# Token halves of an FFN by tile parity, two products of the second weight tile moved into the entry, and a packed halo for the pooling band

## The reference

```python
for i in range(2):
    hn = rms_norm(h, mix_pre_g[i])
    m = multiscale_pool(hn, pool_w, pool_scale) if i == 0 else attention(hn @ w_q, k, v, sinks) @ w_o
    h = h + rms_norm(m, mix_post_g[i])
    f = swiglu(rms_norm(h, ffn_pre_g[i]), w_gate, w_up, w_down)
    h = h + rms_norm(f, ffn_post_g[i])
    h = h + (p[i] @ w_ple_proj[i]) * sigmoid(rms_norm(h, ple_norm_g[i]) @ w_ple_gate[i])
    if i == 0: k, v = shared K (with rotary) and V from rms_norm(h, kv_norm_g)
```

## Time and profile before

| | us |
|---|---|
| median of 3 runs | 1965.93 (1965.68 to 1967.02) |
| the profiled execution | 1965.92 |
| its span | 1964.1 |
| PE busy in the span | 1917.4 |
| mean granted clock | 0.998 of 2.4 GHz |

### The profile page before, as it was taken

One profiled execution on the slowest core, in us unless ns is written; L12 is line 12 of the kernel. 1 busy time (PEld: TensorE's weight loads), 2 busy tenths in 40 slices (PEclk: granted clock), 3 DMA queues, 4 the chain that ended last, 5 costly groups with the idle time before them and its releaser, 6 DMA issues.

```text
span 1964.1 us, 28703 instructions
## 1 busy us (share of the span) xinstructions
PE 1917.4 (98%) x9198; PEld 1573.6 (80%) x9198; DVE 1402.6 (71%) x2382; ACT 905.4 (46%) x1734; POOL 457.5 (23%) x448
## 2 busy tenths in 40 slices
PE   7899999999999999999999999999999999999998
PEld 7778888888888878888866787788888888888787
DVE  5987777777777786565389658777777777777863
ACT  6744444444444453341178545444444444444531
POOL 2312222222222221010046211212122221222310
PEclk9999999999999999999999999999999999999999
DMA  5333332233333350254200213233333223335201
GB/s 201 108 97 104 91 91 87 76 102 91 107 91 91 92 200 22 78 219 172 86 12 2 66 42 123 71 107 92 98 94 91 86 75 106 91 106 176 99 30 67
DMA packets 222055, 188.50 MB, mean 96 GB/s; under 512 B 12192, under 2 KB 199968, under 8 KB 221984
## 3 DMA queue, kind: packets, MB, share of 16 engines
q1 hardware_dynamic: 217712, 183.38, 29.2%
q10 hardware_dynamic: 4272, 4.21, 0.7%
HBM read 166.58 MB, written 20.97 MB: 95 GB/s over the span
## 4 chain that ended last, share of the span: by engine, by line
PE 89%; DVE 6%; issue 2%; ACT 1%; DMA 1%; POOL 1%; SPq 0%; DVEq 0%; ACTq 0%; POOLq 0%
PE ps L827 14%; PE ps L829 14%; PE ps L828 14%; PE ps L315 7%; PE ps L317 7%; PE ps L316 7%; PE ps L925 7%; PE ps L926 7%; PE ps L924 7%; PE ps L1635 2%; PE ps L1716 1%; PE ps L1689 1%; PE ps L389 1%; PE ps L632 1%; DVE t_lo L1261 1%
## 5 line engine op out<-in xcount | busy, mean ns | idle before, releaser
L1249 DVE TENSOR_TENSOR H<-H,ps 128x512 f32<-128x512 f32 x496 | 328.0, 686 | 112.5 <-PE ps L926 111.7
L1111 POOL TENSOR_TENSOR s_raw<-s_raw,a_raw 128x512 f32<-128x512 f32 x66 | 87.5, 1327 | 766.4 <-DVE s_lo L1162 651.0
L827 PE MATMUL ps<-t_hi,s_hi 128*128 128x512 f32 x528 | 206.4, 391 | 8.1 <-DVE t_lo L1261 5.1
L828 PE MATMUL ps<-t_lo,s_hi 128*128 128x512 f32 x528 | 205.5, 389 | 0.0
L829 PE MATMUL ps<-t_hi,s_lo 128*128 128x512 f32 x528 | 205.5, 389 | 0.0
L1000 ACT ACTIVATE m<-ps 128x512 f32<-128x512 f32 x44 | 26.4, 600 | 265.7 <-PE ps L829 263.3
L827 PE MATMUL ps<-b_hi,a_hi 128*128 128x512 f32 x352 | 137.4, 390 | 0.0
L828 PE MATMUL ps<-b_lo,a_hi 128*128 128x512 f32 x352 | 137.3, 390 | 0.0
L829 PE MATMUL ps<-b_hi,a_lo 128*128 128x512 f32 x352 | 137.2, 390 | 0.0
L924 PE MATMUL ps<-wd_hi,d_ab_hi 128*128 128x512 f32 x336 | 130.7, 389 | 0.0
L925 PE MATMUL ps<-wd_lo,d_ab_hi 128*128 128x512 f32 x336 | 130.7, 389 | 0.0
(11 more groups left out here) (293 smaller groups left out, 5022.8 us busy)
## 6 DMA issues: line engine op xcount, KB each, us to landing
a_raw<-in_w_ff_gate SPq DMA_DIRECT2D x88, 256.0 KB, 2.9
a_raw<-in_w_ff_up SPq DMA_DIRECT2D x88, 256.0 KB, 3.0
s_raw<-in_w_ff_up SPq DMA_DIRECT2D x88, 256.0 KB, 2.9
s_raw<-in_w_ff_gate SPq DMA_DIRECT2D x88, 256.0 KB, 3.1
wd_raw<-in_w_ff_down SPq DMA_DIRECT2D x44, 512.0 KB, 4.3
residual_spill<-H SPq DMA_DIRECT2D x16, 512.0 KB, 2.6
raw<-in_w_ple_gate SPq DMA_DIRECT2D x16, 512.0 KB, 6.0
back<-residual_spill SPq DMA_DIRECT2D x16, 512.0 KB, 5.8
```

The source lines that it names most:

```text
L827: pe.matmul(ps[:, bank, :], w[0], x[0], start=fresh and k == 0, stop=False, skip_group_check=not fresh)
L828: pe.matmul(ps[:, bank, :], w[0], x[1], start=False, stop=False, skip_group_check=not fresh)
L1111: eng.tensor_tensor(form_raw(name), W_RAW[name][:, :, :], form_raw(other) if other != "A21" else W_RAW["A21"][:, :, :], op).then_inc(summe ...
L1249: dve.tensor_tensor(dst, dst, src, ALU.add).then_inc(F["summed"], 1)
```

## The change

1. `pool_band` keeps the 8 band products. The 16 last rows of each normed tile are copied by a DMA into a packed tile `halo` (partition 8r+c holds row r of channel chunk c), and two matmuls with 64 columns each add them to all chunks of a bank; the constant `band_halo` replaces `band_before` and is 128 KB instead of 32. The DMA of tile 0 is issued by ACT, the others by SP: those of tiles 1 and 2 after the loads of A11, A12 and A21, the others one behind each spill. PE waits for the halo between the band products and the two new ones.
2. The FFN's token halves are the even and the odd tiles. Every even tile is worked as one of the first half was, every odd tile as one of the second. The rows of H, the spills, the PLE's slots and the output follow (`rows_of`).
3. Entry: A11 and A12 of (0, 0) are cut into pieces, tiles 0, 2, 4 first and tile 6 later; A11 and A12 of (0, 1) are done in the entry too, in banks and buffers of their own, loaded ahead (S1 also). `keep_busy` of 12 is gone. Tile (0, 1) then runs S2, S3, S1, A22, S4 (`ffn_pe_second`). ACT's and DVE's orders of both tiles are rewritten.
4. The load loop of the PLE embeddings is unrolled, and ACT's silu of the second half stands at the end of a weight tile instead of at the start of the next; the pool gain's load counts on another semaphore.

```diff
 ORDER = ("A11", "S3", "S2", "A12", "S1", "A22", "S4")
-ORDER_FIRST = ("A11", "A12", "S3", "S2", "S1", "A22", "S4")
+
+ENTRY = (("A11 begun", 0), ("A11", 0), ("A12", 0), ("A11", 1), ("A12", 1), ("S3", 0), ("S2", 0), ("S1", 0), ("A22", 0), ("S4", 0),
...
         inner.append(near / np.float32(w) - (s == t))
-        before.append(((t + P - s < w) / np.float32(w))[:, :LONGEST])
+        before.append(((t + P - s < w) / np.float32(w))[P - LONGEST:, :LONGEST])
+    halo = np.zeros((P, 2, HALF // KD), np.float32)
+    for c in range(KD):
+        at_ = (c % 4) * LONGEST
+        halo[c::KD, c // 4, at_:at_ + LONGEST] = before[c // 2]
     inv = (1.0 / (10000.0 ** (np.arange(0, HEAD, 2, dtype=np.float32) / np.float32(HEAD)))).astype(np.float32)
...
-                act.activation(piece(t_raw[4], n), ps[:, 7, :], ACT.Copy).then_inc(FN["raw"], 1)
+            if p == 0:
+                act.activation(piece(t_raw[1], i), ps[:, 6, :], ACT.Copy)
+                act.activation(piece(t_raw[4], i), ps[:, 7, :], ACT.Copy).then_inc(FN["raw"], 1)
             else:
-                act.activation(piece(t_raw[3], n - 4), ps[:, 6, :], ACT.Copy)
-                act.activation(piece(xb["b22"][0], n - 4), ps[:, 7, :], ACT.Copy).then_inc(FN["hi"], 1)
+                act.activation(piece(t_raw[3], i), ps[:, 6, :], ACT.Copy)
+                act.activation(piece(xb["b22"][0], i), ps[:, 7, :], ACT.Copy).then_inc(FN["hi"], 1)
...
                 band = B["band_first"] if first else B["band_inner"]
                 o = banks(0)[:, c * P:(c + 1) * P]
-                last = pe.matmul(o, pool_xn[p][:, c * P:(c + 1) * P], band[:, w, :], start=True, stop=first)
-                if not first:
-                    last = pe.matmul(o[:, 0:LONGEST], pool_xn[1 - p][:, c * P:(c + 1) * P], B["band_before"][:, w, :],
-                                     start=False, stop=True)
+                last = pe.matmul(o, pool_xn[p][:, c * P:(c + 1) * P], band[:, w, :], start=first or c % 4 == 0, stop=True,
+                                 skip_group_check=not first and c % 4 > 0)
+            if not first:
+                pe.wait_ge(halo_loaded[1 - p], 16 * (i + p))
+                for b in range(2):
+                    o = ps[:, b, :].rearrange("p (c t) -> p c t", c=4)[:, :, 0:LONGEST]
+                    last = pe.matmul(o, halo[1 - p][:, :], B["band_halo"][:, b, :].rearrange("p (c t) -> p c t", c=4),
+                                     start=False, stop=True, skip_group_check=True)
             last.then_inc(s["turned"][p], 1)
             if first:
 
                 for w in range(12):
                     pe.matmul(ps[:, 6, 0:P], B["band_first"][:, w % 4, :], B["band_first"][:, w % 4, :], start=True, stop=True)
+
+        def halo_move(eng, t):
+
+            i, p = t // 2, t % 2
+            eng.wait_ge(s_pool["xn"][p], s_pool.done("xn", i))
+            eng.dma_start(halo[p][:, :], pool_xn[p][P - LONGEST:, :]).then_inc(halo_loaded[p], 16)
 
         def pool_square_sum(act, i, p):
             s = s_pool
...
+
+        def as_form(x):
+            return x.rearrange("p a c -> p (a c)").rearrange("p (k c) -> p k c", k=4)
+
+        ahead_hi = {"A11": as_form(Z["d_ac_hi"][:, :, :]), "A12": as_form(Z["d_ab_lo"][:, 0:2, :])}
+        ahead_lo = {"A11": as_form(Z["d_ac_lo"][:, :, :]), "A12": as_form(Z["d_ab_lo"][:, 2:4, :])}
+        ahead_raw = {"A11": as_form(Z["d_ac_raw"][:, :, :]), "A12": as_form(Z["d_ab_raw"][:, 2:4, :]),
+                     "S1": as_form(Z["s1_ahead"][:, 0:2, :])}
...
+
+            if is_first(g, t):
+                return 4 if b == 3 else b
+            if is_second(g, t):
+                return 3 if b == 0 else b + 4
+            return b
 
         m7, up0_last, act_late = Z["m7"], Z["up0_last"], ACT_LATE
...
 
             g, t, s = 0, 0, S[("pool", "o")[L]]
+            early, late = slice(0, 3), slice(3, 4)
             pe.wait_ge(*ready("A11", L, g, t))
+            pe.wait_ge(FN["lo"], done(TILES * L + 4))
             if L == 1:
                 pe.wait_ge(FN["ssum"], done(TILES * L + TILES - 2))
-            ffn_pe_prime(pe, "A11", 1)
-            ffn_product(pe, "A11", L, g, t)
-            fn_turn(pe, L, PAIRS - 1, 0)
+            if L == 1:
+                fn_turn(pe, L, PAIRS - 1, 0)
+            ffn_pe_prime(pe, "A11", early, 1)
+            ffn_product(pe, "A11", L, g, t, early)
             pe.wait_ge(s["added"][0], s.done("added", PAIRS - 1))
-            ffn_pe_prime(pe, "A12", 2)
+            pe.wait_ge(*ready("A12", L, g, t))
+            ffn_pe_prime(pe, "A12", early, 2)
+            pe.wait_ge(F["copied"], copied_early(L))
+            ffn_product(pe, "A12", L, g, t, early)
+            if L == 0:
+                fn_turn(pe, L, PAIRS - 1, 0)
+            ffn_product(pe, "A11", L, 0, 1, early)
+            pe.wait_ge(FN["lo"], done(TILES * L + TILES - 2))
+            ffn_pe_prime(pe, "A12", late, 1, 2)
+            ffn_product(pe, "A11", L, g, t, late)
+            pe.wait_ge(s["added"][1], s.done("added", PAIRS - 1))
+            ffn_pe_prime(pe, "A12", slice(0, 4), 5)
+            fn_turn(pe, L, PAIRS - 1, 1)
             pe.wait_ge(F["copied"], nth_copy(0, L, g, t))
-            ffn_product(pe, "A12", L, g, t)
-            fn_turn(pe, L, PAIRS - 1, 1)
-            keep_busy(pe, 12, 3)
+            ffn_product(pe, "A12", L, g, t, late)
+            ffn_product(pe, "A11", L, 0, 1, late)
+            pe.wait_ge(F["copied"], nth_copy(0, L, 0, 1))
+            ffn_product(pe, "A12", L, 0, 1)
             pe.wait_ge(F["t"], 4 * L + 1)
             ffn_product(pe, "S3", L, g, t)
             pe.wait_ge(F["t"], 4 * L + 2)
@@ -866,8 +942,19 @@
             ffn_product(pe, "A22", L, g, t)
             pe.wait_ge(FN["lo"], done(TILES * L + TILES - 1))
             pe.wait_ge(F["up1"], 1 + tau(L, g, t) + 1)
-            pe.wait_ge(*ready("S4", L, g, t))
-            ffn_pe_prime(pe, "S4", 5)
+            ffn_product(pe, "S4", L, g, t)
+
+        def ffn_pe_second(pe, L):
+
+            g, t = 0, 1
+            pe.wait_ge(*ready("S2", L, g, t))
+            ffn_pe_prime(pe, "S2", slice(0, 4), 6)
+            for name in ("S2", "S3"):
+                ffn_product(pe, name, L, g, t)
+            pe.wait_ge(F["copied"], nth_copy(2, L, g, t))
+            for name in ("S1", "A22"):
+                ffn_product(pe, name, L, g, t)
+            pe.wait_ge(F["up1"], 1 + tau(L, g, t) + 1)
...
-            copy_first(act, L, g, t)
+            if L == 1:
+                fn_raw(act, L, PAIRS - 1, 0)
+            copy_first(act, L, g, t, "A11 begun")
             if L == 0:
                 first_hi(act, L)
-            fn_raw(act, L, PAIRS - 1, 0)
+                form_hi(act, "A11", L, 0, 1)
+            else:
+                fn_hi(act, L, PAIRS - 1, 0)
             fn_squares(act, L, PAIRS - 1, 1)
+            if L == 0:
+                fn_raw(act, L, PAIRS - 1, 0)
+                fn_hi(act, L, PAIRS - 1, 0)
+            else:
+                form_hi(act, "A11", L, 0, 1)
+            form_hi(act, "A12", L, 0, 1)
+            copy_first(act, L, g, t)
 
             def t_hi(m, pieces):
 
-                n = pieces.stop + 3
+                n = 2 * pieces.stop - 1
                 act.wait_ge(t_step, steps_of(L, n) + {3: 1, 1: 2, 2: 3, 4: 4}[m])
                 act.activation(xb[f"t{m}"][0][:, pieces, :, :], t_raw[m][:, pieces, :, :], ACT.Copy
                                ).then_inc(F["t_hi"], 1)
 
-            for m in (3, 2):
-                t_hi(m, slice(0, 3))
+            t_hi(3, slice(0, 3))
             fn_raw(act, L, PAIRS - 1, 1)
-            for m in (3, 2):
-                t_hi(m, slice(3, 4))
+            copy_first(act, L, 0, 1)
+            t_hi(3, slice(3, 4))
+            t_hi(2, slice(0, 4))
             t_hi(1, slice(0, 4))
...
             t, p, n = 1, (g, 0), following(g, 1)
             gate_silu(act, L, *p, 1)
-            wd_his(act, L, g, (0, 1))
-            copy_first(act, L, g, t)
-            form_hi(act, "A22", L, g, t)
-            wd_his(act, L, g, (2, 3))
-            copy_m7(act, L, g, t)
-            form_hi(act, "S4", L, g, t)
-            copy_u(act, L, g, t)
+            if is_second(g, t):
+                copy_u(act, L, g, t)
+                copy_m7(act, L, g, t)
+                form_hi(act, "A22", L, g, t)
+                form_hi(act, "S4", L, g, t)
+                wd_his(act, L, g, range(4))
+            else:
+                wd_his(act, L, g, (0, 1))
+                copy_first(act, L, g, t)
+                form_hi(act, "A22", L, g, t)
+                wd_his(act, L, g, (2, 3))
+                copy_m7(act, L, g, t)
+                form_hi(act, "S4", L, g, t)
+                copy_u(act, L, g, t)
             if not is_last(g, t):
                 form_hi(act, "A11", L, *n)
             gate_silu(act, L, g, t, 0)
             if not is_last(g, t):
                 form_hi(act, "S3", L, *n)
+                gate_silu(act, L, g, t, 1)
 
 
...
             if L == 0:
```

(37 more changed lines are left out.)

223 lines of the change are left out of this document (134 added, 89 removed), and 3 rows, old and new, of the table ENTRY_LO.

## The result

| | before | after |
|---|---|---|
| median | 1966.09 us (5 runs, 1965.68 to 1967.02) | 1974.19 us (5 runs, 1972.30 to 1979.08) |
| the profiled execution, its span | 1965.92, 1964.1 | 1972.30, 1970.5 |
| first down product, layer 0 and 1 | 134.64, 1248.64 | 137.24, 1254.87 |

The ratio is 1.0046, with a 95% interval of 1.0035 to 1.0057: the change makes the kernel slower, by 8.1 us. The forecast was 1964.3, its range 1958.5 to 1969.5, and slower had a chance of 0.13. The profiled run is the fastest of the five, so the traces alone show 6.4 us of the loss. They show where it is (a place is given by the start of its first row): 2.6 us up to the first down product of layer 0, 0.25 us more up to the last output product of layer 1's attention, 3.4 us from there to layer 1's first down product, and 0.2 us after it.

What follows compares the result with a forecast made beforehand. PE, busy 98% of the span, was taken as the bound, with DVE carrying the pooling stage and FFN entries. Winning 0.25 us in layer 0's entry and 1.3 in layer 1's gave 1.6 us less, 1964.3 us, range 1958.5 to 1969.5.

Steps and rivals of the forecast that it cites:

- part 3: Entry of layer 1's FFN: first down product at 1247.3 against 1248.64, 1.3 us won.
- the same walk: Layer 1's entry stepped through like layer 0's, PE the bound until the last output product; down product 22.6 us after S2'.
- the sum: Both FFN entries together: 0.25 + 1.3 = 1.6 us less than the profiled execution, giving 1964.3 us.
- Part 2's entry: Entry of layer 0's FFN: tmp(7) at 87.4, S3 at 96.2, down product at 134.4 against 134.64, 0.25 us won.
- The halo of tile 1: Pooling stage: its DMA lands at 27.2 behind the weight loads, PE waits 3.7 us; 3.2 us less on another queue.
- Little of it is on the path: Pooling stage: of 1.3 us less PE work a tile, 9 us over 7 tiles, little shortens the time.
- DVE's loop of 15.1 us for two tiles: Pooling stage: DVE is the bound, a pair of tiles takes 15.1 us instead of 16.0; tile 7's post-scale at 80.4.
- The rival by the clock: Layer 0's entry: idle stretches of PE halve the clock, 7.4 us up to S3, giving 1970.3; chance 0.12.
- The third rival: Both FFN entries: the filler products count in full, 2 x 5.44 minus 0.5 us, giving 1955.5; chance 0.10.
- Its own signs: Right: PE waits over 2 us for tile 2's halo, DVE over 3 for A22'; wrong: half clock between 84 and 97.

Runs made afterwards that it cites:

- the kernel at 1963.05: Changed kernel with tile 1's halo by ACT, matmuls ahead of A11 of the second weight tile, and there A22's hi before the copy of m7; 1963.05 us.
- the two kernels of before with a halo: Kernel before with only the packed halo and its two matmuls added; tile 1's halo issued by SP 1966.76 us, by ACT 1963.20 us.
- the filler: Changed kernel with tile 1's halo by ACT and extra matmuls (20 and 16) ahead of A11 of the second weight tile in both layers; 1969.26 us.
- raw of tile 6: Kernel at 1963.05 with ACT's raw copies and his of tile 6 ahead of its squares of tile 7, layer 0's extra matmuls cut to 11; 1960.75 us.
- S4': Kernel at 1960.75 with the second weight tile's raw S4 loaded ahead into its own buffer, and ACT's and DVE's orders changed with it; 1960.59 us.
- DVE's gap: Kernel at 1960.59 with A11's low, S3's sum and two wd lows put ahead of up's sum in DVE's order; 1957.26 us.
- the last halo experiment: Kernel at 1960.75 with tile 1's halo issued by SP behind three weight loads again; 1964.36 us.

## Why the prediction was wrong, by its own steps

The median is 9.9 us over the forecast. Two steps of the prediction failed: part 3, which took layer 1's entry for "the same walk" and had it win 1.3 us where it lost 3.4, and the sum, which has no term for the clock. Part 2's entry and the pooling stage were a little short as well. Of the 9.9 us 2.8 arise up to layer 0's first down product, 4.7 in the entry of layer 1 (1.3 forecast as won, 3.4 lost), 0.4 elsewhere in the profiled run, and 1.9 lie between the profiled run and the median.

**The halo of tile 1: the price right, in part by luck.** Forecast: lands at 27.2, PE waits 3.7 us, 3.2 us lost. Measured: 26.6, 3.08 us, and 3.0 us in the traces; by the medians of narrow kernels 3.6. The wait itself costs 2.2 and the half clock behind it, which the sum did not have, 0.8. That tile 1's post-scale stood at 34.41 and not at 33.65 is neither: it comes 7.8 us behind the start of the halo's matmuls, at half clock (from 26.65) and at the full clock (from 26.69 to 34.45) alike, where the forecast had 6.45. The reason given was a slow landing behind the loads. The transfer takes 6 us on either queue (2.3 to 3.2 us for the halos from 29 us on, when the weight loads have landed); it is late because SP was held 6.05 us in the issue of the load ahead. The rule cited there, of ring order (the Trainium skill, DMA: Bandwidth & Descriptors, Queues, rings and completion order), pointed to the right queue: through ACT the halo did pass A21's load (21.1 against 26.8), and behind it on SP it landed 0.2 us after that load. But as it needs 6 us on either queue, no run here shows whether the order inside a ring delayed it beyond its late issue.

**"Little of it is on the path": wrong.** The shorter band pays 3.4 us up to tile 7's post-scale in the kernel before, 1.6 until tile 1's and 1.8 in the loop behind it, and 3.1 in the changed one (1.9 and 1.2). The forecast had the first part (30.4 for tile 1, without the wait) and not the second. PE's waits for `xt_lo` in the earlier trace rows were read as slack of the band, but `xt_lo` itself waits for the band of its tile.

**DVE's loop of 15.1 us for two tiles: right, its tail by luck.** From tile 1's post-scale at 34.41 to tile 7's at 81.55 are 47.1 us; forecast 46.75. The pair in the middle took 15.0. At the end two terms were off and cancelled: 10.25 us where 9.05 were forecast, then 7.1 where it was 8.25.

**The entry of layer 0: every step a little too short.** `tmp` of tile 7: forecast 87.4, measured 88.74. S3: 96.2 and 97.99. S2': 111.9 and 114.12. Down product: 134.4 and 137.24. The offset is 1.15 us at tile 7's post-scale and grows by 0.2, 0.45, 0.45 and 0.6. The forecast had seen both waits of DVE for ACT, that for tile 6 (3.2 us behind H of tile 7) and that for A22' (low ended 119.0 forecast, 121.6 measured), and had them in its sum. What it did not see is that each is a choice of order: the runs give 2.3 us for the one and 5.0 to 5.8 us in both layers for the other (4.7 in the traces).

**The entry of layer 1, the step that failed most.** From the last output product to the first down product the forecast had 55.1 us, the kernel before has 56.4, the changed one 59.8, and 58.0 where its clock was full (the profile with the halo by ACT). So 1.8 us are the clock, for which "the same walk" used no price, and 2.9 the walk itself. Behind the wait of 1.95 us the clock fell from 1204.7 to 1208.3, and from A11' to the turn of tile 7 it took 5.6 us where 3.4 were forecast. With the clock full (the kernel at 1963.05) S3 comes 1.8 us sooner behind the last output product. The walk's own 2.9 us are, less 0.2 at its start, 0.5 us until A11', 0.5 up to S3, 1.2 up to S2' (a wait of 0.4 for `t_lo` and of 0.7 ahead of S1 that the walk had left out) and 0.5 behind it, with 0.4 more beside the clock between A11' and the turn. That no half clock is shown in layer 1 was true of the one trace; the two kernels of before with a halo have the same wait there and show 0.60 and 0.57 behind it. One trace could not show that such a wait is safe.

**The rival by the clock, at 0.12, is what happened in part,** in the place it named. It gave a low stretch from A11 late to A12' the price of 7.4 us up to S3. In the changed kernel's profile the stretch ended too early for that, at 88.6, and the clock's share is 0.8 us behind the halo and 1.8 in layer 1. In other kernels' profiles it reached past A12': with the halo by ACT, S3 started at 101.47 with 16 us at half clock, and at 94.98 with the filler, 6.5 us that are there in some runs and not in others. That this is also the 1.9 us by which the median lies above the profiled run is an inference: the changed kernel's slower runs have no trace, only their mean clock, 0.993 against 0.996 to 0.997.

**The sum against the runs.** From 1974.2: the halo's issue 4.2, the fillers 0.8, A22' hi with a shorter filler 6.2, raw of tile 6 2.3, S4' 0.2, DVE's gap 3.3: 17 us to 1957.3. The halo alone gave 3.3 of the 8.8 us under the kernel before, halves by parity and the new entry with mended orders the other 5.5 or so. The third rival, that the filler products count in full, had 1955.5, and the last kernel comes near that time by another sum: the rival counts 10.4 us for the entries and nothing for the halo, and half of the 10.4 was reached.

**Its own signs.** PE's wait for the halo (3.08 us), no such wait at later tiles, and DVE's wait for the A22' hi (3.22) came as foretold. So did one of the signs of being wrong, a low clock between 84 and 97 (0.66 in 84 to 88).

## What to carry to other kernels

When products are moved forward to fill a wait, walk the orders of the engines that feed them: an operation written behind a copy that waits for a product holds everything behind it, and one line of order was worth some 5 us here, about what halves by parity and the new entry gave in the end. Price a new idle stretch of PE twice, by its length and by half the clock over what follows it, and put that second price in the sum and not only in a rival. A small transfer whose time matters goes on a queue whose engine isn't held in the issue of a large one.

## What the runs showed of the hardware that was not expected

The length of the low stretch of the clock behind the same wait of 2.5 us differs from run to run: 3.5 us in the changed kernel's profile (85.2 to 88.6) and 16 us or more in three other kernels' profiles. PE was busy for 14.2 of those 16 us, and the clock stayed at 0.50. Nor does such a wait always lower the clock: behind 2.87 us for the halo, and behind 1.67 and 1.93 us for A11' in layer 1 (the halo by ACT; A22's hi first alone), it stayed at 1.00. The filler covers its own place only: in the profile of the last halo experiment the clock fell to 0.53 at 96 to 98, behind a wait of 0.67 us. The Trainium skill (TensorE: Matmul & The Clock Gate, What's actually happening) says, of the start of a kernel, that the number of slow matmuls varies between its runs; in the entries here the runs agree, with spreads of 3.8 to 8.8 us without the filler ahead of A11', of 1.1 to 1.5 with it and the halo by ACT, and of 2.4 and 3.2 with it and the halo by SP.

Matmuls of 128 columns in this format start every 0.112 us (late pieces of A11, 89.15 to 90.5), and of 384 columns every 0.173. The 55.6 ns for 128 columns that the prediction took from the Trainium skill (TensorE: Matmul & The Clock Gate, Wait — 56ns, not 53.3ns?) is half of that, and the row of the transposes was the right one to take.
